# A two-block transformer kernel on one core: gate tiles as split products, their rests on GpSimd, the layer norm one tile sooner

## The chip, the cores and the metric

The kernel runs on one core of one Trainium2 chip. The metric is the device time of one execution in microseconds, as the median of several runs. "Faster" and "slower" are told against the kernel before.

## What is computed

The reference is a float32 network for 256 tokens of width 1024. A first block (a feed-forward part, a mixer with three kinds of attention, a second feed-forward part) is followed by two equal layers. The change touches the mixing stage of these two layers. With `h` the normalised and modulated input of the layer it computes

```python
proj = h @ w_in[l]
u_conv = proj[..., :2 * D_CONV]                      # a: 8 tiles of 128 columns
u_pool = proj[..., 2 * D_CONV:2 * D_CONV + D_POOL]   # p: 4 tiles
gate_a, gate_b = jnp.split(jax.nn.sigmoid(proj[..., 2 * D_CONV + D_POOL:]), N_BRANCHES, axis=-1)  # G: 16 tiles
y_a = conformer_conv_branch(u_conv, conv_w[l], ...)  # a*sigmoid(g), causal depthwise conv of 31 taps, layer norm, silu, matmul
y_b = pool_branch(u_pool, pool_w[l], pool_scale[l])
x = x + g1[:, None, :] * ((gate_a * y_a + gate_b * y_b) @ w_out[l])
```

Behind it stands a mixture of 32 experts, whose weights (192 tiles of 512 KB per layer) are all read from HBM.

## The kernel before, in words

**Weights as a stream.** All weights lie in HBM as tiles of 128 x 1024 float32 (512 KB). `stream()` (line 180) lists them in the order of their use, with a third entry that says whether a tile is split. SyncE loads them in that order (line 753) into a ring of six buffers `raw`; a load of a tile waits until the buffer's last tile has been used: for a split tile until its rest is made (`lo_done`), for a raw one until its product is done (`pe_tile`). Between these loads stand early loads of expert tiles, one beside each of the tiles p and the first gate tiles.

**Split and raw products.** TensorE multiplies rounded numbers (fp32r) in one pass and full float32 in more. A split tile is turned into a high part `whi` (ScalarE's copy, `hi`, line 1651) and a rest `wlo = raw - whi` (VectorE's subtraction, `lo`, line 2105). The activations are split likewise (`hhi`, `hlo`). `product` (line 928) then makes three fp32r products, high x high, high x rest and rest x high, in place of one full product. There are four buffers of each part (`AHEAD = 4`): ScalarE may copy tile n only when the product of tile n - 4 is done, VectorE makes the rest once the copy is there, and TensorE waits for the rest. A raw tile is multiplied as it is: `feature_tile` (line 963) takes `hf` and the loaded tile (line 969) and needs neither ScalarE nor VectorE before the product.

**The mixing stage of a layer.** TensorE goes through 8 tiles a (the first three in step with the activations), 4 tiles p and 16 gate tiles G, each of 8 chunks of 128 x 128 against 256 tokens; a and p are split, G is raw. Then come one split tile `pool`, four split tiles `conv` and eight split tiles `wout`. ScalarE evicts each product (`evac`, line 1662). VectorE in the meantime makes the products a x sigmoid(g) for four groups of channels (line 2658) and the 124 taps of the convolution (`some_taps`, line 2637), one instruction of 256 columns each, with the rests of the tiles a and p between them. After the last tap comes the layer norm: TensorE sums over the channels (line 1452, behind gate tile `LN_MEAN_G`), VectorE subtracts the mean (line 2696), ScalarE squares, TensorE sums again (line 874, behind gate tile `LN_VAR_G`, after a small product for the router, line 1459), a root, VectorE scales (line 2704), ScalarE applies silu and rounds, and VectorE makes the rest (line 2711). Between them VectorE makes the window means of the four pooling groups. While gate tiles 12 to 15 are multiplied, ScalarE and VectorE split the `pool` tile and the first conv tiles. Last, VectorE joins the branches in four steps of two chunks (lines 2718, 2725, 2730, 2733), with one rest of a `wout` tile in each.

**GpSimd** issues five DMAs in the first 421 us and, per layer, waits for a flag of the router and works only if an expert has more tokens than its place holds.

The lines that set the two kinds of products and VectorE's rests inside the taps:

```python
out += [(f"G{l}", m, False) for m in range(16)]     # line 196, in stream()
...
                for m in range(8):
                    lo(NUMBER[START[f"a{l}"] + m] + AHEAD)
                    if m % 2:
                        c = m // 2
                        evacuated(dve, f"a{l}", m)
```

Of the kernel before, what the change touches and what calls it, by code (L numbers as in the profile page):

```python
# [17 lines left out]
F32 = mybir.dt.float32  # L18
# [15 lines left out]
AHEAD = 4  # L34
# [145 lines left out]
def stream():  # L180

    out = [("ffn1", w, True) for w in swiglu_order(FC)]
    out += [("memk", m, True) for m in range(4)] + [("memv", m, True) for m in range(4)]
    out += [("dn", m, True) for m in range(8)] + [("z", m, True) for m in range(4)]
    out += [("dv", m, True) for m in range(4)] + [("kv", m, True) for m in range(4)]
    out += [("v", m, True) for m in range(2)]
    out += [("q", m, True) for m in range(2)] + [("w1", m, False) for m in range(4)] + [("q", m, True) for m in (2, 3)]
    out += [("memq", m, True) for m in range(2)] + [("w1", m, False) for m in range(4, 8)]
    out += [("memq", m, True) for m in (2, 3)]
    out += [("gate", m, True) for m in range(24)]  # L190
    out += [("branch", (m, b), True) for m in range(4) for b in range(3)]
    out += [("wout", m, True) for m in range(DC)]
    out += [("ffn2", w, True) for w in swiglu_order(FC)]
    for l in range(LAYERS):
        out += [(f"a{l}", m, True) for m in range(8)] + [(f"p{l}", m, True) for m in range(4)]
        out += [(f"G{l}", m, False) for m in range(16)]
        out += [(f"pool{l}", 0, True)] + [(f"conv{l}", m, True) for m in range(4)]
        out += [(f"wout{l}", m, True) for m in range(DC)]
        out += [(f"moe{l}", w, False) for w in moe_order()]
    return out  # L200
# [3 lines left out]
SPLITS = [r for r, t in enumerate(STREAM) if t[2]]  # L204
NUMBER = {r: n for n, r in enumerate(SPLITS)}
START = {}
# [157 lines left out]
while len(TAP_ORDER) < 4 * CONV_K:  # L364
    _left = [c for c in range(4) if sum(t[0] == c for t in TAP_ORDER) < CONV_K][:2]
    TAP_ORDER += [(c, sum(t[0] == c for t in TAP_ORDER)) for c in _left]
LN_MEAN_G, LN_VAR_G, SPLIT_G = 10, 11, 16 - AHEAD


NORM_PARTS = [1 if k in (8, 11) else 4 for k in range(8 + 3 * LAYERS)]  # L370
# [142 lines left out]
def program(nc, wstream, ada_d, c_d, consts_d, params_d, x_d, mem_d, rows_d, out_d):  # L513
    with ExitStack() as ctx:
        sems = {}

        def s(name):
            name = SHARED.get(name, (name, 0))[0]
            if name not in sems:
                sems[name] = ctx.enter_context(nc.semaphore(name))  # L520
            return sems[name]

        def after(name, count):

            return SHARED.get(name, (name, 0))[1] + count
# [287 lines left out]
        @block.gpsimd  # L813
        def _(pool):
            pool.wait_ge(s("pe_tile"), 2)
            pool.dma_start(mem_in[:, :], mem_d.rearrange("p c t -> p (c t)")).then_inc(s("mem_loaded"), 16)
            pool.wait_ge(s("pe_tile"), 10)
            pool.dma_start(consts[:, P:], consts_d[:, P:]).then_inc(s("consts_loaded"), 16)
            pool.wait_ge(s("bias_rows"), 1)
            pool.dma_start(rows_d.rearrange("h (j n) c -> (h j) n c", n=HEADS), spread(rt[:, 0:1], (HEADS, BROW), (0, 1))  # L820
                           ).then_inc(s("rows_stored"), 16)
            pool.dma_start(params[:, NFIRST:NPARAM], params_d[:, NFIRST:NPARAM]).then_inc(s("layer_params"), 16)
            pool.wait_ge(s("rows_stored"), 16)

            skew = bass.AP(tensor=rows_d.tensor, offset=P - 1, ap=[[BROW - 1, P], [P * BROW, HEADS], [1, T]])
            pool.wait_ge(s("dn_out"), after("dn_out", 1))
            pool.dma_start(tb[:], skew).then_inc(s("tb_loaded"), 16)

            for l in range(LAYERS):
                pool.wait_ge(s("flag_ready"), after("flag_ready", l + 1))  # L830
                with pool.If(pool.value_load(overflow[0:1, l:l + 1], min_val=0, max_val=1) > 0):
                    pool.wait_ge(s("pe_tile"), START[f"moe{l}"] + 6 * EXPERTS)

                    def unit(u, gu, d, i):
                        if u > 0:
                            pool.wait_ge(s(f"spare_free{l}"), along(u, i, 4))

                        half = slice(512 * (u % 2), 512 * (u % 2) + 512)

                        def tile(r):  # L840
                            at = START[f"moe{l}"] + r
                            src = wstream[at:at + 1, :, half] if i is None else wstream[bass.ds(at + 24 * i, 1), :, half]
                            return src.rearrange("o p c -> (o p) c")
                        for k in range(8):
                            pool.dma_start(gate2[:, 2 * k:2 * k + 2, :].rearrange("p c t -> p (c t)"), tile(gu[k])
                                           ).then_inc(s(f"spare_loaded{l}"), 16)
                        for k in range(4):
                            pool.dma_start(spare_d[:, k % 2, 512 * (k // 2):512 * (k // 2) + 512], tile(d[k])
                                           ).then_inc(s(f"spare_loaded{l}"), 16)
                    spare_units(pool, unit)  # L850
# [797 lines left out]
        def _(act):  # L1648
# [13 lines left out]
            def evac(r, out, bank, func=ACT.Copy):  # L1662
                act.wait_ge(s("pe_tile"), r + 1)
                src = work[bank][:, 0:T]
                if len(out.shape) == 3:
                    src = src.rearrange("p (q f) -> p q f", q=QT)
                assert EVAC[r] == done[0]
                act.activation(out, src, func).then_inc(s("tile_evac"), 1)  # L1668
                done[0] += 1
# [311 lines left out]
            for l in range(LAYERS):  # L1981
# [13 lines left out]
                for m in range(8):  # L1995
# [3 lines left out]
                        act.wait_ge(s("glu_done"), 4 * l + m // 2 - 1)  # L1999
                    evac(r, (pair_a, pair_b)[m % 2][:, (m // 2) % 2, :], m % 4, (ACT.Copy, ACT.Sigmoid)[m % 2])  # L2000
                for m in range(4):
                    evac(START[f"p{l}"] + m, ppad[:, m, 16:16 + T], m % 4)
                for m in range(16):
                    evac(START[f"G{l}"] + m, gate2[:, m, :], m % 4, ACT.Sigmoid)
                    if m == LN_MEAN_G:
                        act.wait_ge(s("ln_centred"), l + 1)
                        act.activation(ln_squares[:, :, :], yconv[:, :, :], ACT.Square).then_inc(s("norm_sq"), 1)
                    elif m == LN_VAR_G:
                        roots(k + 1)
                    if m >= SPLIT_G:  # L2010
                        hi(NUMBER[START[f"pool{l}"]] + m - SPLIT_G)
                    if m == SPLIT_G:
                        act.wait_ge(s("ln_scaled"), l + 1)
                        for c in range(4):
                            a = act.activation(yconv[:, c, :], yconv[:, c, :], ACT.Silu, bias=col(f"ln_b{l}", c),
                                               scale=col(f"ln_g{l}", c))
                        a.then_inc(s("y_silu"), 1)
                        act.wait_ge(s("y_silu"), after("y_silu", l + 1))
                        act.activation(yhi[:, :, :], yconv[:, :, :], ACT.Copy).then_inc(s("y_high"), 1)
# [76 lines left out]
        def _(dve):  # L2096
# [525 lines left out]
            for l in range(LAYERS):  # L2622
# [28 lines left out]
                    tap_at[0] += n  # L2651

                for m in range(8):
                    lo(NUMBER[START[f"a{l}"] + m] + AHEAD)
                    if m % 2:
                        c = m // 2
                        evacuated(dve, f"a{l}", m)
                        dve.tensor_tensor(vpad[:, c, 30:30 + T], pair_a[:, c % 2, :], pair_b[:, c % 2, :], ALU.mult
                                          ).then_inc(s("glu_done"), 1)
                        dve.wait_ge(s("glu_done"), 4 * l + c + 1)  # L2660
                    if m > 0:
                        some_taps(4)
# [41 lines left out]
                dve.tensor_tensor(yconv[:], yconv[:], spread(rstd[:, 0:1], (4, T), (0, 1)), ALU.mult  # L2704
                                  ).then_inc(s("ln_scaled"), 1)
                pooling(3).then_inc(s("pooled"), 1)
                for m in range(SPLIT_G, 16):
                    lo(NUMBER[START[f"pool{l}"]] + m - SPLIT_G)
                    if m == SPLIT_G:
                        dve.wait_ge(s("y_high"), l + 1)  # L2710
                        dve.tensor_tensor(ylo[:], yconv[:], yhi[:].bitcast(F32), ALU.subtract).then_inc(s("y_ready"), 1)
                lo(NUMBER[START[f"pool{l}"]] + AHEAD)

                dve.wait_ge(s("pe_tile"), START[f"pool{l}"] + 1)
                evacuated(dve, f"G{l}", 15)
                for m in range(4):
# [11 lines left out]
                    dve.wait_ge(s("conv_read"), 4 * l + m + 1)  # L2728
                    c = slice(2 * m, 2 * m + 2)
                    dve.tensor_tensor(hf[:, c, :], hf[:, c, :], gate2[:, c, :], ALU.add).then_inc(s("mixed"), 1)  # L2730
                    lo(NUMBER[START[f"conv{l}"] + m] + AHEAD)
                    dve.wait_ge(s("mixed_high"), 4 * l + m + 1)
                    dve.tensor_tensor(hlo[:, c, :], hf[:, c, :], hhi[:, c, :].bitcast(F32), ALU.subtract
# [355 lines left out]
```

## Time and profile before

| | us |
|---|---|
| median of 3 runs | 1586.73 |
| lowest and highest run | 1584.74, 1590.69 |
| profiled execution, its own time | 1583.35 |
| its span | 1581.7 |
| TensorE busy | 1445.7 (91%) |
| VectorE busy | 907.6 (57%) |
| ScalarE busy | 577.4 (37%) |
| GpSimd busy | 3.7 (0%) |

In the profile's rows PE is TensorE, PEld its weight loads, DVE VectorE, ACT ScalarE, POOL GpSimd and SP SyncE. L934 is line 934 of the kernel. Times are us from the span's start unless marked ns. PEclk is the granted TensorE clock as a share of 2.4 GHz. The chain of waits is followed back from the last instruction to what released each; each of its pieces has a start and a length.

### The profile page before, as it was taken

The numbers are of one execution on the slowest core, as the hardware profiler recorded it, in microseconds if no ns is written. First come the engines' busy times: TensorE is split into PE (matmuls) and PEld (weight loads), VectorE is DVE, ScalarE is ACT, GpSimd is POOL, SyncE is SP. The second block draws the span as 40 slices with busy tenths as digits, with TensorE's granted clock in tenths as the row PEclk, the third lists the DMA queues.
The fourth block names the chain that finished last, engine by engine and source line by source line (L and its number), as shares of the span: only waits on it lengthen the run. The fifth ranks groups of instructions, "written<-read, shape, count | busy, mean of one in ns | idle before, by whom it ended". The sixth has DMA issues, their size and how long they took to land.

```text
span 1581.7 us, 26885 instructions
## 1 busy us (share of the span) xinstructions
PE 1445.7 (91%) x10541; PEld 1174.6 (74%) x10553; DVE 907.6 (57%) x1615; ACT 577.4 (37%) x916; POOL 3.7 (0%) x9
## 2 busy tenths in 40 slices
PE   9999999989978899999999999987779999997776
PEld 8999999979877798999999898422217989532222
DVE  6898877684435576888877986210016987410102
ACT  4543346522445554434445153221115143221101
POOL 0000000000000000000000000000000000000000
PEclk9999999999989999999999999999999999899997
DMA  8998854412522344888875558899996749699996
GB/s 303 380 356 310 304 179 147 147 54 107 188 67 95 120 144 163 321 307 299 309 252 192 208 200 346 336 409 409 409 410 258 272 133 378 246 409 409 409 410 252
DMA packets 115803, 420.87 MB, mean 266 GB/s; under 512 B 12944, under 2 KB 13088, under 8 KB 115568
## 3 DMA queue, kind: packets, MB, share of 16 engines
q1 hardware_dynamic: 114624, 414.19, 70.5%
q0 software_dynamic: 1072, 5.20, 0.9%
q8 instruction: 74, 1.21, 0.3%
q14 instruction: 33, 0.27, 0.0%
HBM read 416.71 MB, written 2.62 MB: 265 GB/s over the span
## 4 chain that ended last, share of the span: by engine, by line
PE 68%; DMA 12%; DVE 7%; SPq 5%; ACT 4%; issue 3%; DVEq 0%; ACTq 0%
PE work L934 25%; PE acc L934 12%; PE work L969 7%; SPq L753 5%; PE work L1025 5%; PE work L1570 4%; DMA raw<-wstream_d 3%; DMA over_splits<-wstream_d 3%; DMA hf<-wstream_d 2%; PE work L894 2%; PE work L904 2%; ACT whi L1660 2%; DVE wlo L2110 1%; PE work L1597 1%; DMA over_end<-wstream_d 1%
## 5 line engine op out<-in xcount | busy, mean ns | idle before, releaser
L2110 DVE TENSOR_TENSOR wlo<-raw,whi 128x1024 fp32r<-128x1024 f32 x264 | 321.1, 1223 | 174.6 <-ACT whi L1660 174.1
L1660 ACT ACTIVATE whi<-raw 128x1024 fp32r<-128x1024 f32 x264 | 277.0, 1056 | 278.6 <-PE work L934 190.7
L934 PE MATMUL work<-hhi,whi 128*128 128x256 f32 x1024 | 293.7, 287 | 2.2 <-DVE hlo L2138 1.3
L934 PE MATMUL work<-hlo,whi 128*128 128x256 f32 x1024 | 292.2, 285 | 0.0
L934 PE MATMUL work<-hhi,wlo 128*128 128x256 f32 x1024 | 292.1, 285 | 0.0
L934 PEld LDWEIGHTS work<-hhi,whi 128*128 128x128 f32 x1024 | 198.8, 194 | 4.5 <-DVE wlo L2110 3.0
L934 PEld LDWEIGHTS work<-hlo,whi 128*128 128x128 f32 x1024 | 198.8, 194 | 0.1
L934 PEld LDWEIGHTS work<-hhi,wlo 128*128 128x128 f32 x1024 | 198.6, 194 | 0.0
L2862 DVE TENSOR_TENSOR pair_b<-work,pair_a 128x256 f32<-128x256 f32 x16 | 6.8, 425 | 213.0 <-ACT pair_a L2065 213.0
L2221 DVE SCALAR_TENSOR_TENSOR ada_tiles<-ada_tiles,c_act 128x1024 f32<-128x1024 f32 x96 | 116.3, 1220 | 0.6 <-DMA ada_tiles<-ada_d 0.5
L969 PE MATMUL work<-hf,raw 128*128 128x256 f32 x512 | 111.5, 379 | 0.0
L969 PEld LDWEIGHTS work<-hf,raw 128*128 128x128 f32 x512 | 97.1, 190 | 13.1
L1025 PE MATMUL work<-hhi,whi 128*128 128x256 f32 x288 | 86.7, 301 | 21.0 <-ACT gates L1668 17.8
L934 PE MATMUL acc<-ahi,whi 128*128 128x256 f32 x352 | 99.1, 281 | 2.8 <-DVE alo L2256 2.8
L2646 DVE SCALAR_TENSOR_TENSOR yconv<-vpad,params,yconv 128x256 f32<-128x256 f32 x240 | 99.4, 479 | 1.4
L934 PE MATMUL acc<-alo,whi 128*128 128x256 f32 x352 | 99.6, 283 | 0.0
L934 PE MATMUL acc<-ahi,wlo 128*128 128x256 f32 x352 | 99.4, 282 | 0.0
L1025 PE MATMUL work<-hhi,wlo 128*128 128x256 f32 x288 | 84.6, 294 | 0.0
L1025 PE MATMUL work<-hlo,whi 128*128 128x256 f32 x288 | 84.2, 292 | 0.0
L2048 ACT ACTIVATE xg<-work,mod,gscale 128x256 f32<-128x256 f32 x56 | 29.0, 562 | 140.0 <-PE work L1505 140.0
L1025 PEld LDWEIGHTS work<-hhi,whi 128*128 128x128 f32 x288 | 57.0, 198 | 26.3 <-issue 23.7
L2858 DVE TENSOR_REDUCE rt<-work 32x1 f32<-32x2 f32 x64 | 10.0, 156 | 113.0 <-ACT selectT L2056 111.5
(483 smaller groups left out, 2690.4 us busy)
## 6 DMA issues: line engine op xcount, KB each, us to landing
raw<-wstream_d SPq DMA_DIRECT2D x376, 512.0 KB, 4.8
ada_tiles<-ada_d SPq DMA_DIRECT2D x96, 512.0 KB, 5.2
over_splits<-wstream_d SPq DMA_DIRECT2D x80, 512.0 KB, 15.2
over_select<-wstream_d SPq DMA_DIRECT2D x48, 512.0 KB, 14.8
over_end<-wstream_d SPq DMA_DIRECT2D x24, 512.0 KB, 15.2
spare_d<-wstream_d SPq DMA_DIRECT2D x24, 512.0 KB, 14.7
over_pool<-wstream_d SPq DMA_DIRECT2D x22, 512.0 KB, 15.1
hf<-wstream_d SPq DMA_DIRECT2D x20, 512.0 KB, 15.1
```

What stands on the lines that cost most here:

```text
L753: sp.dma_start(tiles[slot][:], src).then_inc(s(landed(slot)), 16)
L894: mm = pe.matmul(work[bank][:, q:q + 1], hf[:, m, q * P:(q + 1) * P], ones[:, 0:1], start=(m == 0 and q == 0), stop=(m == DC - 1), skip_gr ...
L904: pe.matmul(work[bank][:, :], zero[:, :], spread(zero[:, 0:1], (512,), (0,)), start=True, stop=True)
L934: mm = pe.matmul(out, a, b, start=(start and k == 0), stop=(stop and k == n - 1), skip_group_check=skip)
L969: mm = pe.matmul(work[bank][:, 0:T], h[:, c * P:(c + 1) * P], hf[:, c, :], start=(c == 0), stop=(c == DC - 1))
L1025: mm = pe.matmul(bank[:, 0:T], ((h, h, l)[k % 3])[:, c * P:(c + 1) * P], ((hhi, hlo, hhi)[k % 3])[:, c, :], start=(k == 0), stop=(k == 23))
L1570: mm = pe.matmul(work[0][SLOTS * e:SLOTS * e + SLOTS, :], xg[:, p // 2 % 2, k, a:a + SLOTS], w[:, e % 2 * 512:(e % 2 + 1) * 512], start=(k ...
L1660: act.activation(whi[n % AHEAD][:], tiles[SLOT[SPLITS[n]]][:], ACT.Copy).then_inc(s("hi_done"), 1)
L2048: return act.activation(out, src, ACT.Identity, bias=mod[:, b:b + 1], scale=gscale[:, g:g + 1])
L2110: dve.tensor_tensor(wlo[n % AHEAD][:], tiles[SLOT[SPLITS[n]]][:], whi[n % AHEAD][:].bitcast(F32), ALU.subtract).then_inc(s("lo_done"), 1)
L2221: dve.scalar_tensor_tensor(ada_tiles[:, k, :], ada_tiles[:, k, :], 1.0, c_act[:], ALU.mult, ALU.mult, accum_out=out).then_inc(s("ada_done" ...
L2646: ins = dve.scalar_tensor_tensor(yconv[:, c, :], vpad[:, c, i:i + T], w, yconv[:, c, :], ALU.mult, ALU.add)
```

## The change

The gate tiles of both layers become split tiles. So each needs a copy on ScalarE (`hi` before its eviction, as for the tiles p now too) and a rest. The rests of the tiles from a4 to conv3 (29 per layer: 4 a, 4 p, 16 G, pool, 4 conv) are made by GpSimd in a loop `rests`; VectorE's calls for 13 tiles go. VectorE still makes the rests of a0 to a3 and of the `wout` tiles; before the first of these it waits until GpSimd has ended its last. The mean of the layer norm is summed behind gate tile 9 in place of 10, the variance behind 10 in place of 11.

```diff
--- before.py
+++ after.py
@@ -193,7 +193,7 @@
     out += [("ffn2", w, True) for w in swiglu_order(FC)]
     for l in range(LAYERS):
         out += [(f"a{l}", m, True) for m in range(8)] + [(f"p{l}", m, True) for m in range(4)]
-        out += [(f"G{l}", m, False) for m in range(16)]
+        out += [(f"G{l}", m, True) for m in range(16)]
         out += [(f"pool{l}", 0, True)] + [(f"conv{l}", m, True) for m in range(4)]
         out += [(f"wout{l}", m, True) for m in range(DC)]
         out += [(f"moe{l}", w, False) for w in moe_order()]
@@ -364,7 +364,7 @@
 while len(TAP_ORDER) < 4 * CONV_K:
     _left = [c for c in range(4) if sum(t[0] == c for t in TAP_ORDER) < CONV_K][:2]
     TAP_ORDER += [(c, sum(t[0] == c for t in TAP_ORDER)) for c in _left]
-LN_MEAN_G, LN_VAR_G, SPLIT_G = 10, 11, 16 - AHEAD
+LN_MEAN_G, LN_VAR_G, SPLIT_G = 9, 10, 16 - AHEAD
 
 
 NORM_PARTS = [1 if k in (8, 11) else 4 for k in range(8 + 3 * LAYERS)]
@@ -826,7 +826,16 @@
             pool.wait_ge(s("dn_out"), after("dn_out", 1))
             pool.dma_start(tb[:], skew).then_inc(s("tb_loaded"), 16)
 
+            def rests(first, end):
+
+                pool.wait_ge(s("lo_done"), first)
+                for n in range(first, end):
+                    pool.wait_ge(s("hi_done"), n + 1)
+                    pool.tensor_tensor(wlo[n % AHEAD][:], tiles[SLOT[SPLITS[n]]][:], whi[n % AHEAD][:].bitcast(F32),
+                                       ALU.subtract).then_inc(s("lo_done"), 1)
+
             for l in range(LAYERS):
+                rests(NUMBER[START[f"a{l}"]] + AHEAD, NUMBER[START[f"wout{l}"]])
                 pool.wait_ge(s("flag_ready"), after("flag_ready", l + 1))
                 with pool.If(pool.value_load(overflow[0:1, l:l + 1], min_val=0, max_val=1) > 0):
                     pool.wait_ge(s("pe_tile"), START[f"moe{l}"] + 6 * EXPERTS)
@@ -1999,16 +2008,16 @@
                         act.wait_ge(s("glu_done"), 4 * l + m // 2 - 1)
                     evac(r, (pair_a, pair_b)[m % 2][:, (m // 2) % 2, :], m % 4, (ACT.Copy, ACT.Sigmoid)[m % 2])
                 for m in range(4):
+                    hi(NUMBER[START[f"p{l}"] + m] + AHEAD)
                     evac(START[f"p{l}"] + m, ppad[:, m, 16:16 + T], m % 4)
                 for m in range(16):
+                    hi(NUMBER[START[f"G{l}"] + m] + AHEAD)
                     evac(START[f"G{l}"] + m, gate2[:, m, :], m % 4, ACT.Sigmoid)
                     if m == LN_MEAN_G:
                         act.wait_ge(s("ln_centred"), l + 1)
                         act.activation(ln_squares[:, :, :], yconv[:, :, :], ACT.Square).then_inc(s("norm_sq"), 1)
                     elif m == LN_VAR_G:
                         roots(k + 1)
-                    if m >= SPLIT_G:
-                        hi(NUMBER[START[f"pool{l}"]] + m - SPLIT_G)
                     if m == SPLIT_G:
                         act.wait_ge(s("ln_scaled"), l + 1)
                         for c in range(4):
@@ -2651,7 +2660,6 @@
                     tap_at[0] += n
 
                 for m in range(8):
-                    lo(NUMBER[START[f"a{l}"] + m] + AHEAD)
                     if m % 2:
                         c = m // 2
                         evacuated(dve, f"a{l}", m)
@@ -2704,12 +2712,8 @@
                 dve.tensor_tensor(yconv[:], yconv[:], spread(rstd[:, 0:1], (4, T), (0, 1)), ALU.mult
                                   ).then_inc(s("ln_scaled"), 1)
                 pooling(3).then_inc(s("pooled"), 1)
-                for m in range(SPLIT_G, 16):
-                    lo(NUMBER[START[f"pool{l}"]] + m - SPLIT_G)
-                    if m == SPLIT_G:
-                        dve.wait_ge(s("y_high"), l + 1)
-                        dve.tensor_tensor(ylo[:], yconv[:], yhi[:].bitcast(F32), ALU.subtract).then_inc(s("y_ready"), 1)
-                lo(NUMBER[START[f"pool{l}"]] + AHEAD)
+                dve.wait_ge(s("y_high"), l + 1)
+                dve.tensor_tensor(ylo[:], yconv[:], yhi[:].bitcast(F32), ALU.subtract).then_inc(s("y_ready"), 1)
 
                 dve.wait_ge(s("pe_tile"), START[f"pool{l}"] + 1)
                 evacuated(dve, f"G{l}", 15)
@@ -2728,6 +2732,8 @@
                     dve.wait_ge(s("conv_read"), 4 * l + m + 1)
                     c = slice(2 * m, 2 * m + 2)
                     dve.tensor_tensor(hf[:, c, :], hf[:, c, :], gate2[:, c, :], ALU.add).then_inc(s("mixed"), 1)
+                    if m == 0:
+                        dve.wait_ge(s("lo_done"), NUMBER[START[f"wout{l}"]])
                     lo(NUMBER[START[f"conv{l}"] + m] + AHEAD)
                     dve.wait_ge(s("mixed_high"), 4 * l + m + 1)
                     dve.tensor_tensor(hlo[:, c, :], hf[:, c, :], hhi[:, c, :].bitcast(F32), ALU.subtract
```

## Rows read from the trace of the kernel before

**Rows 1.** The page: span, then busy time, share and instructions of the engines

```profile
span 1581.7 us, 26885 instructions
...
PE 1445.7 (91%) x10541; PEld 1174.6 (74%) x10553; DVE 907.6 (57%) x1615; ACT 577.4 (37%) x916; POOL 3.7 (0%) x9
```

**Rows 2.** The chain of waits in both layers' mixing stages: start, us, what

```profile
840.30 34.55 PE work L934 x288
874.86 37.99 PE work L969 x176
912.85 1.73 PE work L1452 x8
914.57 3.45 PE work L969 x16
918.02 1.71 PE work L1459 x16
...
921.54 13.81 PE work L969 x64
935.35 2.83 PE acc L934 x24
938.18 11.31 PE work L934 x96
...
1243.13 37.99 PE work L969 x176
```

**Rows 3.** Windows: length, busy time of the engines, clock, DMA share, GB/s

```profile
874.86:912.85 37.99, 37.99 (x177) 33.44 (x177) 37.48 (x94) 4.23 (x11) 0.00 (x0) 1.00 0.52 184
...
975.10:1000.00 24.90, 22.26 (x162) 15.49 (x166) 15.26 (x65) 8.39 (x16) 0.00 (x0) 0.93 0.60 227
1000.00:1198.40 198.40, 159.38 (x988) 55.56 (x982) 22.30 (x59) 35.47 (x69) 0.00 (x0) 0.95 1.03 408
```

**Rows 4.** VectorE's timeline in the first layer: start, length, what [idle before, releaser]

```profile
852.33 0.43 DVE L2658 TENSOR_TENSOR vpad<-pair_a,pair_b 128x256 f32<-128x256 f32 x1 [0.47 <-ACT pair_b L1668]
...
871.09 12.49 DVE L2646 SCALAR_TENSOR_TENSOR yconv<-vpad,params,yconv 128x256 f32<-128x256 f32 x31
...
890.21 21.66 DVE L2646 SCALAR_TENSOR_TENSOR yconv<-vpad,params,yconv 128x256 f32<-128x256 f32 x52
912.02 0.53 DVE L2668 TENSOR_TENSOR vpad<-params,gscale 128x144 f32<-128x144 f32 x2 [0.15 <-DVE yconv L2646]
...
930.87 1.23 DVE L2711 TENSOR_TENSOR yp<-yconv,yp 128x1024 fp32r<-128x1024 f32 x1 [0.38 <-ACT yp L2019]
```

**Rows 5.** ScalarE's timeline in the first layer

```profile
848.31 1.06 ACT L1660 ACTIVATE whi<-raw 128x1024 fp32r<-128x1024 f32 x1 [3.60 <-PE work L934]
...
864.40 0.36 ACT L1668 ACTIVATE pair_b<-work 128x256 f32<-128x256 f32 x1
...
878.35 0.38 ACT L1668 ACTIVATE gate<-work 128x256 f32<-128x256 f32 x1 [3.07 <-PE work L969]
```

**Rows 6.** Instruction groups of VectorE from 852.3 to 912: busy us, mean ns

```profile
L2646 DVE SCALAR_TENSOR_TENSOR yconv<-vpad,params,yconv 128x256 f32<-128x256 f32 x120 | 49.7, 478 | 0.7
L2110 DVE TENSOR_TENSOR wlo<-raw,whi 128x1024 fp32r<-128x1024 f32 x6 | 7.3, 1220 | 0.0
```

**Rows 7.** GpSimd's instruction groups over the span, the longest and a constant

```profile
L827 POOL DMA_DIRECT2D tb<-bias_rows_d x1 | 0.9, 909 | 334.3 <-DVEq L2516 334.3
...
L3081 POOL MEMSET const-float32-1.0<- 128x1 f32 x1 | 0.1, 98 | 0.0
```

**Rows 8.** VectorE's reciprocal of the layer norm, in its timeline

```profile
922.80 1.75 DVE L2123 RECIPROCAL rstd<-std 128x256 f32<-128x256 f32 x1 [0.48 <-ACT std L1693]
```

**Rows 9.** VectorE's timeline in the first step of the joining

```profile
940.51 0.87 DVE L2718 SCALAR_TENSOR_TENSOR hf<-acc,params,gate 128x256 f32<-128x256 f32 x2
...
944.07 0.69 DVE L2733 TENSOR_TENSOR hlo<-hf,hhi 128x512 fp32r<-128x512 f32 x1
```

**Rows 10.** Windows of a gap in the expert stage and of the routing

```profile
1039.00:1040.00 1.00, 0.00 (x0) 0.00 (x0) 0.00 (x0) 0.00 (x0) 0.00 (x0) 1.00 1.02 406
...
988.00:990.00 2.00, 2.00 (x11) 2.00 (x11) 1.69 (x10) 1.13 (x2) 0.00 (x0) 0.50 0.01 4
```

## The prediction

> **What bounds the kernel now.** I read four views of the layer that begins near 840 us; the second layer repeats them 368.3 us later with the same lengths, as its first gate part shows beside layer one's [rows 2]. First the page: TensorE is busy for 91% of the span [rows 1]. Then the chain of waits [rows 2]: from 840.30 to 949.49 us every piece is TensorE's own work and no other engine stands in it. The reader is to see two tile prices there. Twelve split tiles (a, p) take 34.55 us, 2.879 us each; eleven raw gate tiles take 37.99 us, 3.454 us each. Third the windows [rows 3]: during the gate tiles the clock is 1.00 and DMA half idle (0.52), and behind the mixing stage the expert loads run at 408 GB/s and bound the next 198 us, but only after a stretch at 0.60, where they wait for buffers and not for bandwidth. Fourth VectorE's timeline [rows 4]: its last tap ends at 911.87, just before TensorE asks for it at 912.85. So both engines are close to the path, and the change shortens both.
>
> **Part 1, gate tiles split.** Each of 16 gate tiles goes from 3.454 to 2.879 us: 16 x 0.575 = 9.2 us less on TensorE per layer. The two price tags are of the same engine at the same clock, so this term is firm. ScalarE gets 16 more copies of 1.06 us [rows 5]; it sits idle 3.07 us before each gate eviction [rows 5] and they fit there (2.88 - 0.38 leaves 2.5). A load of a weight tile into a buffer that held a gate tile now waits for that tile's rest and no longer for its product, so no tile comes later; SyncE's queue gets no new instruction.
>
> **Part 2, rests on GpSimd.** VectorE loses 13 of its 1.22 us rests per layer, of which six lie inside the tap stretch, 7.3 us [rows 6]. How long GpSimd takes for one 128x1024 subtraction T no row shows: in this trace GpSimd only issues a few DMAs and sets constants [rows 7]. Bounds: the same instruction on VectorE, 1.22 us [rows 6], and the dearest element in the trace, the reciprocal's 1.75 us for 256 elements, 7.0 us for 1024 [rows 8]. I take 2.4 us, twice the row with the same operation and shape, as the nearer end; what matters is only on which side of three limits it falls. (a) The rest of a4: ScalarE's copy runs 848.31 to 849.37 [rows 5], the product needs it when a3 ends, 874.86 - 8 x 2.879 = 851.83, so 2.46 us are free: cost 0, at T = 2.88 about 0.4. (b) Steady state: T must stay under 2.88 us, or GpSimd sets the pace. (c) The new wait of VectorE at the first mixed pair: ScalarE copies the last conv tile after the pool product, GpSimd ends some 3.5 us behind that product (4.6 if it is one rest behind), while VectorE gets to its wait 4.4 us behind it (conv0's 2.83, then 0.9 and 0.7). Cost 0 to 0.2 us, and queued behind it are only VectorE's first rest for the out projection and its second half, which TensorE needs 11.3 us after the pool product [rows 2]. The first pair takes from 940.51 to 944.76 today [rows 9]; the slack stays.
> The Trainium skill ("GPSIMD Engine Reference", section "3.1 Elementwise — side-by-side cycle accounting") measures such an operation at 1.96 times VectorE's time for twice this length. By that ratio an estimate from our 1.22 us row is 2.4 us, and the sum stays as it is; no run here shows it yet.
>
> **Part 3, VectorE's taps and the earlier layer norm.** The last product of the a stage that the taps need is evicted at 864.40 + 0.36 = 864.76 [rows 5]. Before it VectorE has from 852.33 only 24 taps and three gate products (24 x 0.41 + 3 x 0.45 = 11.2 us), so it stands ready at 863.5; today the rests keep it busy until 871.09 [rows 4]. The 100 taps behind it take 911.87 - 871.09 = 40.8 us [rows 4]. So the taps end at 864.8 + 0.45 + 40.8 = 906.0, 5.9 us sooner. TensorE finishes gate tile 9, where the mean now stands, at 874.86 + 10 x 2.88 = 903.7. It waits 2.4 us, with nothing else in its queue to do: +2.4 us. From the mean on the length is unchanged: today 22.50 us to the last gate tile (mean 1.73, one tile 3.45, router row and squares 3.52, four tiles 13.81) [rows 2]; after it 1.73 + 2.88 + 3.52 + 5 x 2.88 = 22.5. VectorE's chain from the last tap to the split layer norm output takes 932.1 - 911.9 = 20.2 us [rows 4], so it ends near 926, and TensorE asks at 931.4. Not on the path.
>
> **Sum.** Per layer -9.2 + 2.4 = -6.8 us; the expert stage starts so much sooner, and as its loads wait for buffers that TensorE frees, it shifts whole. Two layers: -13.6 us. The profiled execution took 1583.35 us, which gives 1569.8; it lies 3.4 us under the median of the runs, so I forecast a median of 1573. Own range of this case: 1565 (hardly any wait before the mean, 4.8 us better) to 1579 (0.4 us at a4, and the wait costing clock). On the clock: a gap of 1.2 us leaves it at 1.00, but in the routing stretch with its thin products it falls to the 1.2 GHz level [rows 10]; a few us at that level after the 2.4 us wait would cost 1 to 3 us per layer.
>
> **Rival 1, slower: the two engines can't both read.** Place: the 100 taps, each with two inputs from SBUF, while GpSimd reads two others. If a rest holds VectorE for h us, 21 rests (a5 to gate 13) come before the mean is free; 1.3 us of that falls into VectorE's idle time at 863.5. Taps end at 906.0 + 21h - 1.3. The gain of 9.2 is used up when they end at 912.85, at h = 0.39 us. With h = 1.22 they end at 930.3, TensorE waits 26.6 us, +17.4 per layer: 1583.35 + 34.9 + 3.4 = 1621.6. For it: VectorE's rate on two inputs, 0.41 us for 256 columns, is one column a cycle with little to spare, and its path has no slack left (2.4 us negative). Against it: no row of this trace shows two engines slowing each other, ScalarE and VectorE run side by side all along.
> The Trainium skill ("SBUF — State Buffer", "Summary: rules for kernel authors") speaks against this change: a VectorE instruction with two SBUF inputs and a GpSimd one that reads SBUF exclude each other, the later one waiting for the whole of the earlier. With the ratio above h would be 2.4 us and the estimate 1671; the trace has no GpSimd arithmetic to agree or not. I give this rival 0.27, and a weak form with h of 0.2 to 0.5 another 0.05, which ends within 0.5%.
>
> **Rival 2: GpSimd sets the pace.** For T above 2.88 us, 29 rests cost 29 x (T - 2.88) per layer, in place of the 2.4 us wait: break-even at T = 3.20. T between 3.06 and 3.33 gives within 8 us of no change; T = 3.45 gives +7.3 per layer, 1601. For it: the range of T reaches to 7.0. Against: only the reciprocal is so slow. Chance 0.18, 0.10 of it without a measurable difference and 0.08 slower.
>
> **Rival 3: the gain is swallowed.** If the expert stage is paced by bandwidth from further back (the loads of the mixing stage included), 6.8 us sooner on TensorE only lengthen its waits there, and the time stays at 1587. Against it the 0.60 stretch before the saturated one [rows 3]. Chance 0.05.
>
> **How the numbers follow.** What a measurement can tell here is about 0.5%, 7.9 us. The forecast with its variants has 0.45, all faster by more than that. Within 0.5%: 0.05 + 0.10 + 0.05 = 0.20. Slower: 0.27 + 0.08 = 0.35. The likeliest single case gives the number, 1573. The range goes from 1563, a bit under the own range, to 1650, which holds rival 1 up to h of about 1.9 and rival 2 up to T of 4.3; it leaves out the dearer third of rival 1 and the far end of rival 2.
>
> **What would show it.** Raw products are gone from line 969; the gate tiles take 2.88 us each in the chain. GpSimd has 58 subtractions. Right: VectorE's taps stay at 0.41 us apart and end 5.9 us sooner, and TensorE has one wait of 2 to 3 us per layer before the mean, on VectorE. Rival 1: taps in the same 480 ns shape take far longer in mean or with gaps, the last ending after 912, and a long TensorE wait in front of the mean. Rival 2: gaps between all tiles from a4 on, ended by GpSimd, with starts more than 2.88 us apart. Rival 3: the gate stretch shorter as said, and DMA waits in the expert stage longer by as much. Any of these would make the forecast wrong, as would an expert stage that doesn't shift whole.

## The result and the profile after

| | before | after |
|---|---|---|
| median, us | 1587.36 | 1670.67 |
| lowest and highest, us | 1584.74, 1590.69 | 1666.98, 1671.49 |
| span of the profiled execution | 1581.7 | 1669.8 |
| TensorE busy | 1445.7 | 1446.2 |
| VectorE busy | 907.6 | 980.0 |

The change makes the kernel slower: ratio 1.0524, interval 1.0507 to 1.0542, five runs of each. The forecast of 1573 with its range up to 1650 was wrong, in sign too. Rival 1 gave 1622 if a rest takes h = 1.22 us from VectorE, and 1671 with h = 2.4.

The page of after, its engines [rows 1] and the slices of the clock (tenths of 2.4 GHz):

```profile
span 1669.8 us, 27499 instructions
...
PE 1446.2 (87%) x10797; PEld 1180.3 (71%) x10809; DVE 980.0 (59%) x1589; ACT 606.4 (36%) x948; POOL 148.8 (9%) x67
...
PEclk8999999899989999999999599999979859999996
```

VectorE lost 26 rests of 1.22 us and yet is busy 72 us longer. TensorE has the same busy time in a longer span, so it waits somewhere. The waits of TensorE by line (us in total, times, longest) say where:

```profile
PE work L1461 <- DVEq L2673: 88.5, 2, 44.3
```

That is the mean of the layer norm, waiting for the taps, 44.2 us per layer. The instruction groups of after say what the taps suffer:

```profile
L2655 DVE SCALAR_TENSOR_TENSOR yconv<-vpad,params,yconv 128x256 f32<-128x256 f32 x240 | 170.6, 775 | 1.4
L834 POOL TENSOR_TENSOR wlo<-raw,whi 128x1024 fp32r<-128x1024 f32 x58 | 145.0, 2531 | 838.3 <-ACT whi L1669 837.8
L2666 DVE TENSOR_TENSOR vpad<-pair_a,pair_b 128x256 f32<-128x256 f32 x8 | 15.6, 1956 | 13.0 <-ACT pair_b L1677 13.0
```

The taps, 478 ns in [rows 6], have a mean of 775 ns. But a mean hides the pattern; the two timelines of the first layer show it. GpSimd's (start, length, what):

```profile
854.77 17.38 POOL L834 TENSOR_TENSOR wlo<-raw,whi 128x1024 fp32r<-128x1024 f32 x7 [435.00 <-ACT whi L1669]
875.77 38.04 POOL L834 TENSOR_TENSOR wlo<-raw,whi 128x1024 fp32r<-128x1024 f32 x15 [3.62 <-ACT whi L1669]
```

and VectorE's, against [rows 4]:

```profile
857.63 2.19 DVE L2666 TENSOR_TENSOR vpad<-pair_a,pair_b 128x256 f32<-128x256 f32 x1 [6.61 <-ACT pair_b L1677]
859.86 2.39 DVE L2651 TENSOR_SCALAR yconv<-vpad,params 128x256 f32<-128x256 f32 x1
...
888.74 20.36 DVE L2655 SCALAR_TENSOR_TENSOR yconv<-vpad,params,yconv 128x256 f32<-128x256 f32 x8
...
932.71 21.67 DVE L2655 SCALAR_TENSOR_TENSOR yconv<-vpad,params,yconv 128x256 f32<-128x256 f32 x52
```

Read these three steps together. While GpSimd has no pause (875.77 to 913.81, 38.04 / 15 = 2.54 us a rest), eight taps take 20.36 us, 2.54 us each: **one tap per rest**. When GpSimd is idle, 52 taps take 21.67 us, 0.417 each, as before. A rest thus takes 2.54 - 0.417 = 2.12 us from VectorE. The Trainium skill ("SBUF — State Buffer", section "Who interferes with whom") says that the two engines share one pair of ports, as an exclusive lock held for a whole instruction; these timelines agree, with 2.54 us for 256 columns that need 0.42.

The chain of after, from the first tiles of the layer to the out projection, answers to [rows 2]:

```profile
845.54 8.65 PE work L943 x72
...
954.49 3.64 PE work L1461 x8
958.12 2.88 PE work L943 x24
...
962.47 1.97 PE work L1468 x16
964.45 3.22 PE work L883 x8
967.67 14.63 PE work L943 x120
982.29 2.83 PE acc L943 x24
985.12 11.31 PE work L943 x96
```

**Where the time went.** The layer begins at 845.54 in place of 840.30, 5.2 us of the profiled execution that lie ahead of the first instruction that the change touches. (In the traces here this start lies between 840.3 and 846.8; one trace per kernel doesn't tell whether that belongs to the kernel or to the execution.) With that taken off, the mean begins 954.49 - 912.85 - 5.24 = 36.4 us later than before, and from the mean to the end of gate tile 15 it takes 982.29 - 954.49 = 27.8 us in place of 22.5. Both together are 41.7 us per layer; 2 x 41.7 + 5.2 = 88.6, against 88.1 us by which the spans differ. The medians differ by 83.3 us, which is 2 x 41.7 nearly to the tenth. The pieces from conv0 to the out projection have the lengths of before.

The 5.3 us behind the mean are a second cost of the wait. The windows of after (length, busy PE, PEld, DVE, ACT, POOL, clock, DMA share, GB/s):

```profile
920.00:940.00 20.00, 0.00 (x0) 0.00 (x0) 19.93 (x52) 0.00 (x0) 0.00 (x0) 0.50 0.00 0
...
954.00:958.00 4.00, 3.51 (x9) 2.86 (x10) 2.87 (x9) 0.00 (x0) 0.00 (x0) 0.52 0.00 0
958.00:961.00 3.00, 3.00 (x25) 2.79 (x23) 2.62 (x6) 1.06 (x1) 0.00 (x0) 1.00 0.04 8
```

TensorE stands still, the granted clock falls to its 1.2 GHz level, and the mean runs at that level: 3.64 us in place of 1.73.

### The profile page after: what moved, and what is told of

Same layout as the page of the kernel before. It is cut to its first block, busy times and chain, and to the rows that moved or that the text cites. A ratio compares the mean times of both kernels' runs of the same rounds, so it can differ in the third digit from the quotient of the medians.

```text
span 1669.8 us, 27499 instructions
## 1 busy us (share of the span) xinstructions
PE 1446.2 (87%) x10797; PEld 1180.3 (71%) x10809; DVE 980.0 (59%) x1589; ACT 606.4 (36%) x948; POOL 148.8 (9%) x67
## 4 chain that ended last, share of the span: by engine, by line
PE 57%; DVE 16%; DMA 11%; SPq 7%; ACT 5%; issue 4%; DVEq 0%; ACTq 0%
PE work L943 24%; PE acc L943 11%; DVE yconv L2655 10%; SPq L753 7%; PE work L1034 5%; DMA hf<-wstream_d 3%; PE work L1579 3%; DMA raw<-wstream_d 2%; DMA ln_squares<-wstream_d 2%; ACT whi L1669 2%; PE work L903 2%; PE work L913 1%; PE work L1606 1%; DMA c_act<-wstream_d 1%; DMA over_vpad<-wstream_d 1%
## 5 line engine op out<-in xcount | busy, mean ns | idle before, releaser
L1669 ACT ACTIVATE whi<-raw 128x1024 fp32r<-128x1024 f32 x296 | 310.9, 1057 | 315.2 <-PE work L943 228.8
L2119 DVE TENSOR_TENSOR wlo<-raw,whi 128x1024 fp32r<-128x1024 f32 x238 | 289.2, 1223 | 163.0 <-ACT whi L1669 162.4
L943 PE MATMUL work<-hhi,whi 128*128 128x256 f32 x1280 | 368.7, 288 | 2.9 <-POOL wlo L834 0.9
L943 PE MATMUL work<-hlo,whi 128*128 128x256 f32 x1280 | 364.8, 285 | 0.0
L943 PE MATMUL work<-hhi,wlo 128*128 128x256 f32 x1280 | 364.4, 285 | 0.0
L943 PEld LDWEIGHTS work<-hhi,whi 128*128 128x128 f32 x1280 | 248.7, 194 | 6.6 <-DVE wlo L2119 2.5
L943 PEld LDWEIGHTS work<-hlo,whi 128*128 128x128 f32 x1280 | 248.6, 194 | 0.5
L943 PEld LDWEIGHTS work<-hhi,wlo 128*128 128x128 f32 x1280 | 248.3, 194 | 0.0
L834 POOL TENSOR_TENSOR wlo<-raw,whi 128x1024 fp32r<-128x1024 f32 x58 | 145.0, 2531 | 838.3 <-ACT whi L1669 837.8
L2655 DVE SCALAR_TENSOR_TENSOR yconv<-vpad,params,yconv 128x256 f32<-128x256 f32 x240 | 170.6, 775 | 1.4
L1034 PE MATMUL work<-hhi,whi 128*128 128x256 f32 x288 | 88.1, 306 | 21.0 <-ACT gates L1677 17.8
L1034 PE MATMUL work<-hhi,wlo 128*128 128x256 f32 x288 | 85.8, 298 | 0.0
L1034 PE MATMUL work<-hlo,whi 128*128 128x256 f32 x288 | 85.7, 298 | 0.0
L1034 PEld LDWEIGHTS work<-hhi,whi 128*128 128x128 f32 x288 | 58.2, 202 | 26.1 <-issue 24.0
```

The costliest lines, as they stand in the source:

```text
L834: pool.tensor_tensor(wlo[n % AHEAD][:], tiles[SLOT[SPLITS[n]]][:], whi[n % AHEAD][:].bitcast(F32), ALU.subtract).then_inc(s("lo_done"), 1)
L943: mm = pe.matmul(out, a, b, start=(start and k == 0), stop=(stop and k == n - 1), skip_group_check=skip)
L1034: mm = pe.matmul(bank[:, 0:T], ((h, h, l)[k % 3])[:, c * P:(c + 1) * P], ((hhi, hlo, hhi)[k % 3])[:, c, :], start=(k == 0), stop=(k == 23))
L1669: act.activation(whi[n % AHEAD][:], tiles[SLOT[SPLITS[n]]][:], ACT.Copy).then_inc(s("hi_done"), 1)
L2119: dve.tensor_tensor(wlo[n % AHEAD][:], tiles[SLOT[SPLITS[n]]][:], whi[n % AHEAD][:].bitcast(F32), ALU.subtract).then_inc(s("lo_done"), 1)
L2655: ins = dve.scalar_tensor_tensor(yconv[:, c, :], vpad[:, c, i:i + T], w, yconv[:, c, :], ALU.mult, ALU.add)
```

## The experiments

Experiments 5 and 7 start from the kernel before, the others from the kernel after. Ratios are to the kernel before, timed on the same chip.

**1. Gate tiles raw again, the other rests on GpSimd.** The mean stands behind tile 10 again, and GpSimd makes the 13 rests of a layer that VectorE made before.

```diff
-        out += [(f"G{l}", m, True) for m in range(16)]
+        out += [(f"G{l}", m, False) for m in range(16)]
...
-LN_MEAN_G, LN_VAR_G, SPLIT_G = 9, 10, 16 - AHEAD
+LN_MEAN_G, LN_VAR_G, SPLIT_G = 10, 11, 16 - AHEAD
...
-                    hi(NUMBER[START[f"G{l}"] + m] + AHEAD)
```

> The changed kernel with the gate tiles raw again and the mean behind tile 10: GpSimd makes 13 rests per layer, 8 of them (a4 to p3) while the taps run. Theory L (a GpSimd subtraction and a VectorE instruction with SBUF inputs exclude each other, one VectorE instruction passing per rest): the after trace has the taps end 43.2 us later than my 906.0 for 21 rests, 2.06 us each; 8 rests give 906.0 + 8 x 2.1 - 1.3 = 921.5, so TensorE waits some 8.7 us before the mean and the time is about 1587 + 17 = 1604. Theory G (the gate tiles' splitting is what costs: ScalarE's copies, the clock or the order of waits): then this kernel is at 1587, and its taps stay 480 ns.

1611.21 us, 1.0138 (1.0114 to 1.0163). The groups:

```profile
L2655 DVE SCALAR_TENSOR_TENSOR yconv<-vpad,params,yconv 128x256 f32<-128x256 f32 x240 | 119.6, 565 | 1.4
...
L834 POOL TENSOR_TENSOR wlo<-raw,whi 128x1024 fp32r<-128x1024 f32 x26 | 63.7, 2481 | 856.8 <-ACT whi L1669 856.8
```

Slower with not one gate tile split: eight rests of a layer stand beside the taps, and TensorE waits 5.2 us before each mean. So the use of GpSimd alone costs, and with 8 of its instructions beside the taps in place of 22 it costs less. The wait had been expected at 8.7 us and the time near 1604. Behind the wait the mean takes 3.78 us in place of 1.73 and the tile 4.52 in place of 3.45. Wait and both make 8.3 us per layer; the time rose by 22 us in all, so some 5 us are not explained.

**2. GpSimd only writes.** It writes zeros in place of the rests; the low part of 29 weight tiles per layer is left out of the computation.

```diff
-                    pool.tensor_tensor(wlo[n % AHEAD][:], tiles[SLOT[SPLITS[n]]][:], whi[n % AHEAD][:].bitcast(F32),
-                                       ALU.subtract).then_inc(s("lo_done"), 1)
+                    pool.memset(wlo[n % AHEAD][:].bitcast(F32), 0.0).then_inc(s("lo_done"), 1)
```

> The changed kernel in which GpSimd fills the rest tiles with zeros in place of the subtraction (the 58 rests are left out of the result), so that it writes the same 128x1024 but reads nothing. Theory L in the form of a shared input path: taps back at 480 ns, TensorE's wait before the mean near 2.4 us, time 1573. Theory L with any GpSimd work holding VectorE: each fill of about 1 us holds a tap by its length, taps' mean above 550 ns and the time above 1600. Theory G: near 1670, as nothing in the waits changes.

1578.81 us, 0.9945 (0.9924 to 0.9967), 92 us below after. Its groups, then its waits of TensorE:

```profile
L2654 DVE SCALAR_TENSOR_TENSOR yconv<-vpad,params,yconv 128x256 f32<-128x256 f32 x240 | 99.1, 479 | 1.4
...
L834 POOL MEMSET wlo<- 128x1024 f32 x58 | 55.4, 954 | 832.5 <-ACT whi L1668 832.5
```

```profile
PE work L1460 <- DVEq L2672: 5.0, 2, 2.5
...
PE work L1467 <- ACT gate L1676: 3.0, 2, 1.5
```

An engine that reads nothing beside the taps leaves them at 479 ns. This is nearly the forecast's case, with the collision gone (GpSimd is also quicker than forecast, 0.95 us in place of 2.4), and it lets the rest of the sum be read: TensorE waits 2.5 us before the mean, where the forecast had 2.4. But the gain is not 13.6 us, it is 8.7 (0.0055 x 1586, with the interval 5.2 to 12.1); why is seen in its chain:

```profile
914.69 0.92 ACT ln_squares L2017
915.65 1.05 ACT whi L1668
916.71 0.28 ACT gate L1676
917.03 1.98 PE work L1467 x16
919.00 2.94 PE work L882 x8
921.94 14.89 PE work L942 x120
```

The router's product waits 1.5 us for the eviction of gate tile 10. That eviction stands in ScalarE's queue behind the squares, and now also behind the new copy of a tile, 1.05 us, that a raw tile did not need. Then the variance takes 2.94 us in place of 1.81, in a window with the clock at 0.59 (919 to 922). From the mean, at 910.7, to the end of the gates at 936.83 it takes 26.1 us, not 22.5: 3.6 per layer that the forecast did not have. With them its sum would give 13.6 - 2 x 3.6 = 6.4 us, inside the interval.

**3. Shorter instructions on GpSimd.** The same rests in four parts of 256 columns.

```diff
+                    for j in range(4):
+                        a = slice(j * T, (j + 1) * T)
+                        ins = pool.tensor_tensor(wlo[n % AHEAD][:, a], tiles[SLOT[SPLITS[n]]][:, a],
+                                                 whi[n % AHEAD][:, a].bitcast(F32), ALU.subtract)
+                    ins.then_inc(s("lo_done"), 1)
```

> The changed kernel with each GpSimd rest made in four instructions of 256 columns. Theory L, exclusion for the length of one instruction: no tap longer than about 1.2 us (a quarter of 2.5 plus its own 0.48) where now they reach 2.6, four taps pass per rest; GpSimd's turns take 4 x (0.65 + 0.41) = 4.2 us per tile, over TensorE's 2.88, so TensorE has gaps before tiles from a5 on; the sum of both engines' work until the mean is the same, so time within 1650 to 1690. Rival (the two engines share bandwidth and both slow down evenly): taps keep their long shape of around 2 us.

1664.76 us, 1.0481 (1.0453 to 1.0509). Its group on GpSimd and its waits of TensorE:

```profile
L836 POOL TENSOR_TENSOR wlo<-raw,whi 128x256 fp32r<-128x256 f32 x232 | 194.0, 874 | 777.8 <-ACT whi L1672 777.8
```

```profile
PE work L1464 <- DVEq L2676: 58.7, 2, 29.4
...
PE work L946 <- POOL wlo L836: 12.7, 34, 0.6
```

And its taps in VectorE's timeline, beside the eight of after:

```profile
873.97 7.00 DVE L2658 SCALAR_TENSOR_TENSOR yconv<-vpad,params,yconv 128x256 f32<-128x256 f32 x8
```

A tap now takes 7.00 / 8 = 0.875 us, as long as one GpSimd instruction of 0.874. So the hold lasts one GpSimd instruction, whatever its length, and one VectorE instruction passes between two of them. Four holds of 0.875 - 0.417 = 0.46 us take 1.8 us per rest from VectorE in place of 2.12, so the total hardly falls. The wait before the mean shrinks to 29.4 us mostly because TensorE comes to it later: four parts together take GpSimd 4 x 0.87 = 3.5 us, longer than the 2.88 us of a product, so GpSimd now sets the pace of the gate tiles: rival 2's mechanism, made by the experiment.

**4. The running sum of the taps in PSUM.** A tap then has one input in SBUF and one in PSUM, and all the rests stay on GpSimd. The last tap of a channel group writes SBUF.

```diff
-                            ins = dve.scalar_tensor_tensor(yconv[:, c, :], vpad[:, c, i:i + T], w, yconv[:, c, :],
+                            ins = dve.scalar_tensor_tensor(yconv[:, c, :] if i == CONV_K - 1 else acc_c[:, c, :],
+                                                           vpad[:, c, i:i + T], w, acc_c[:, c, :],
```

> The changed kernel with the taps' running sum in PSUM (the part of acc that is free then), only the last tap of each group writing to SBUF: each tap has one SBUF input in place of two, GpSimd's subtractions stay. Theory L with the second SBUF input as what collides: taps of about 480 ns, only the four gate products (two SBUF inputs) are held for up to 2.5 us each; TensorE's wait before the mean 2 to 10 us; time 1573 to 1588. If any SBUF read of VectorE collides, the time stays near 1670. Theory G: 1670 too.

1594.36 us, 1.0039 (1.0018 to 1.0060), 76 us below after. Its group of taps, and its timeline of VectorE:

```profile
L2655 DVE SCALAR_TENSOR_TENSOR acc<-vpad,params,acc 128x256 f32<-128x256 f32 x232 | 95.7, 484 | 1.3
```

```profile
858.87 2.19 DVE L2667 TENSOR_TENSOR vpad<-pair_a,pair_b 128x256 f32<-128x256 f32 x1 [6.58 <-ACT pair_b L1677]
861.10 0.55 DVE L2651 TENSOR_SCALAR acc<-vpad,params 128x256 f32<-128x256 f32 x1
...
869.22 1.68 DVE L2667 TENSOR_TENSOR vpad<-pair_a,pair_b 128x256 f32<-128x256 f32 x1
870.93 3.23 DVE L2655 SCALAR_TENSOR_TENSOR acc<-vpad,params,acc 128x256 f32<-128x256 f32 x8
...
886.81 0.48 DVE L2655 SCALAR_TENSOR_TENSOR yconv<-vpad,params,acc 128x256 f32<-128x256 f32 x1
```

GpSimd still takes 2464 ns for each of its 58 rests, and the taps run through it at 484 ns. What has two inputs in SBUF, the product a x sigmoid(g), is held as before, up to 2.19 us in place of 0.43 [rows 4]; TensorE waits 6.1 us per layer, and the time is above the 1573 to 1588 that were expected. The last row tells input from output: the last tap of a group reads its sum from PSUM and writes SBUF, a rest of GpSimd runs from 885.87 to 888.27, and the tap still takes 0.48 us. So what holds a tap is its second input in SBUF, not its output there.

**5. The control: the same edit of the taps in the kernel before.**

> Control for e4: the kernel before (raw gates, all rests on VectorE, nothing on GpSimd) with the taps' running sum in PSUM. If the PSUM form costs or gains nothing by itself (taps of 484 ns in e4 against 480), the time is 1587 within 0.5%; if it is what brought e4 back by 76 us, this kernel would be far faster than 1587.

1585.56 us, 0.9987 (0.9969 to 1.0006), taps 484 ns. The form in PSUM is neutral without GpSimd; all that it gains in experiment 4 is the collision.

**6. The layer norm where it was.** After, with the mean behind tile 10 and the variance behind 11 (one line, as in experiment 1).

> The changed kernel with part 3 undone: mean behind gate tile 10, variance behind 11. Theory L: the mean still waits for the last tap; TensorE does one more tile (2.9 us) before the wait, but GpSimd one more rest (2.1 us held) too, so the gain per layer is below 1 us: 1666 to 1672. If the earlier mean were a cost of its own of several us, the time would fall by over 5 us.

1668.26 us, 1.0506 (1.0474 to 1.0538), against 1.0524 (1.0507 to 1.0542) of after; TensorE waits 43.6 us before the mean. The earlier mean has no measurable part in the loss.

**7. The gates split, no GpSimd.** VectorE makes all the rests, 16 more than before, four taps between two of them. The mean stands behind tile 13, and ScalarE's silu behind tile 15, so that TensorE has other work meanwhile.

```diff
+                for j in range(16):
+                    lo(NUMBER[START[f"G{l}"]] + j)
+                    some_taps(4)
```

> Part 1 alone: gate tiles split, all rests on VectorE (16 more per layer, each followed by four taps), GpSimd unused, the mean behind tile 13, where VectorE can be ready. Theory L says VectorE's time is what pays in either case, 1.13 us per rest of its own against 2.1 us held by GpSimd: taps end near 852.3 + 53 + 24 x 1.13 = 932 in place of 954 (after), and the chain of the layer norm, 20 us, then sets the start of conv near 952 in place of 938: +14 per layer, time 1610 to 1622, slower than before but about 50 us faster than the changed kernel. If the splitting as such cost what the change lost, this would be near 1670.

1625.61 us, 1.0228 (1.0200 to 1.0257), a little above the span that was expected and 45 us below after. Its chain, inside the gates:

```profile
907.02 1.13 DVE wlo L2110
908.15 1.59 DVE yconv L2646 x4
...
934.40 3.78 PE work L1452 x8
```

A rest on VectorE costs VectorE 1.13 us; a rest on GpSimd costs VectorE 2.12. Handing the work over takes nearly twice as much from the engine that it was to relieve.

**8. GpSimd with one input.** It copies the raw tile in place of subtracting; the result is no rest, so the values of the layers are others, the router's too.

```diff
+                    pool.tensor_copy(wlo[n % AHEAD][:], tiles[SLOT[SPLITS[n]]][:]).then_inc(s("lo_done"), 1)
```

> The changed kernel in which GpSimd copies the raw tile into the rest tile in place of the subtraction (the rests are left out of the result): one input is read, 128x1024, and as much written. The hold per rest should be the copy's own length: if the copy takes 1.0 to 1.3 us, taps meet it with up to 1.5 us, 21 x (1.1 - 0.4) = 15 to 20 us later taps in place of 43, time 1600 to 1620. If reading one tensor does not hold VectorE, the taps stay at 480 ns and the time is that of e2, 1579.

2918.22 us, 1.8404. Its groups on GpSimd show why this time says nothing on the question:

```profile
L853 POOL DMA_DIRECT2D gate<-wstream_d x256 | 137.1, 538 | 1293.6 <-PE acc L1648 874.4 <-PE work L1605 256.4 <-issue 154.4
...
L834 POOL CAST wlo<-raw 128x1024 fp32r<-128x1024 f32 x58 | 65.4, 1128 | 634.8 <-ACT whi L1668 634.6
```

The DMAs of line 853 belong to the path for an expert with too many tokens; in after GpSimd has its 58 rests and nine other instructions, and none of these. Only the mixing stage can be read, in VectorE's groups and in the chain:

```profile
L2654 DVE SCALAR_TENSOR_TENSOR yconv<-vpad,params,yconv 128x256 f32<-128x256 f32 x240 | 129.5, 602 | 1.4
```

```profile
858.09 1.32 DVE yconv L2654
...
859.44 1.19 DVE yconv L2654
...
860.66 0.49 DVE yconv L2654
```

A copy of 1.13 us holds a tap too, up to 1.32 us: one read by GpSimd is enough. The hold is shorter because the instruction is. And since this copy and the zeros of experiment 2 (1.13 and 0.95 us) are of nearly one length and write the same tile, it is GpSimd's read that makes the difference, not its length or its write.

**9 and 10. What is left of the idea.** Taps in PSUM, GpSimd's rests only up to gate tile 15, VectorE makes those of pool and conv as before. The mean stands behind tile 10 in the first, behind 11 in the second.

```diff
-                rests(NUMBER[START[f"a{l}"]] + AHEAD, NUMBER[START[f"wout{l}"]])
+                rests(NUMBER[START[f"a{l}"]] + AHEAD, NUMBER[START[f"pool{l}"]])
```

> e4 (split gates, taps in PSUM, GpSimd) with two edits: the mean behind tile 10, and GpSimd's rests end with gate tile 15 (24 per layer), VectorE again makes those of pool and conv as before the change, so that GpSimd is quiet while VectorE runs the window means and the joining. Theory L: the taps end where they do in e4 (9.8 us behind my 900-line: 6.1 us of wait becomes 3.2), no held instruction in the window means but those beside the rests of tiles 14 and 15, no wait of VectorE in the joining: 5 to 8 us per layer better than e4, 1594 - 10..16 = 1578 to 1584, just under the kernel before. If it stays at 1590 or above, the layer norm's chain of VectorE and ScalarE is the bound and not GpSimd's holds.

> e7 with the mean behind gate tile 11 and the variance behind 12. TensorE's wait before the mean falls to about 0.3 us, which saves its clock, but the chain from the last tap to the layer norm's output (20 us and more) then ends after TensorE has done the pool product, so up to 4 us per layer are lost there: within 4 us of e7, either side.

Behind 10: 1583.41 us, 0.9969 (0.9954 to 0.9983), a little faster than before and the lowest median here of the kernels that compute the whole reference. It is not clear of experiment 5, the kernel before with its taps in PSUM (1585.56, on the same chip; the runs of the two overlap). So a gain from split gates and GpSimd as such is not shown. Behind 11: 1590.36, 1.0020 (0.9995 to 1.0044), no difference from before, and 7 us above the first where at most 4 had been expected. The chain of the first:

```profile
914.42 2.45 PE work L1461 x8
916.88 3.96 PE work L943 x24
...
924.35 11.72 PE work L943 x96
```

Its gates are split and cheap, yet the wait before the mean is 3.2 us, and the mean and the tile behind it run partly at the lower clock, 2.45 and 3.96 us in place of 1.73 and 2.88. So 1.8 of the 9.2 us per layer go there, on top of the wait. With the mean one tile later TensorE waits 0.4 us for the taps, but the chain then runs through VectorE's layer norm, and in it through a window mean that is held beside the last rest of GpSimd, for 2.32 us in place of 0.29:

```profile
913.73 2.32 DVE L2696 TENSOR_SCALAR rt<-pair_a 128x256 f32<-128x256 f32 x1
```

From the first tile of the layer to conv0 it takes 94.7 us with the mean behind 11, 91.5 with the mean behind 10, and 95.1 in the kernel before: the gain is returned.

## Why the prediction was wrong

- **The step that failed is in Part 2:** GpSimd's rests were costed at nothing for VectorE, so that Part 3 could end the taps at 906.0. They ended at 954.4, and TensorE waited 44.2 us in place of 2.4. Nothing in the trace of before could show it, as the text said; the step should have carried h as an unknown cost of its own, bounded from nothing to the whole of T. Instead the two halves of that range were split into forecast and rival, and the rival that named place, price and rule got 0.27 against 0.45. The argument used against it, that VectorE and ScalarE run side by side, is about another pair of engines and says nothing of this one.
- **Rival 1** came true in kind. Its formula with h = 2.12 and the profiled execution's 5.2 us gives 906.0 + 44.5 - 1.3 + 5.2 = 954.4, the end that was measured. Its 1671 fits so well partly by chance: h was 2.12 and not 2.4 (one tap passes per rest), 12 us less over two layers, and the 5.3 us per layer behind the mean, which it had not, brought 11 back.
- **Part 1** held: 2.88 us per gate tile. It missed one spot, where the new copy delays an eviction that TensorE waits for (1.5 us, experiment 2).
- **T** was taken as 2.4 us; GpSimd takes 2.40 beside taps that don't collide (experiment 9, from 880.76 on) and 2.54 beside those that do. So (b) held and rival 2 fell. The ratio of the Trainium skill ("GPSIMD Engine Reference", section "3.1 Elementwise — side-by-side cycle accounting"), 1.96, agrees with this trace: 2.40 against 1.22 us. No wait of VectorE at the first mixed pair showed up as a cost, so (c) held; but the pair is ready 3.8 us before TensorE needs it and no longer 4.7, so the slack did not quite stay.
- **Part 3:** the 2.4 us wait was right once the collision was gone (2.5, experiment 2). The stretch behind the mean was mis-sized: 26.1 us, not 22.5. The clock after a short wait had been given 1 to 3 us per layer in words, but was left out of the sum.
- **Rival 3** fell: the expert stage shifted nearly whole. From conv0 to the next layer's first tile it takes 275.6 us in after and 273.4 in experiment 2, whose mixing stage is 3.0 us shorter than before, in place of 273.2. In experiments 1, 4 and 10 it takes 277.5 to 277.8; why is not shown.
- **The lower end of the own range**, 1565, is 4.8 us below the profiled execution's 1569.8 and not below the median's 1573; on that footing it is 1568. The 1563 of the stated range leans on it; the outcome lies at the other end.
- Even without the collision the gain would have been 8.7 us, 0.5%, not 13.6: just what a measurement here can tell.

Left open: a version that also keeps the four products a x sigmoid(g) from reading two SBUF inputs was not tried; by experiment 4 they are held for some 4 x 1.2 us per layer.

## What to carry to other kernels

Before work goes to an idle engine, ask what each instruction of the busy one reads at the same time: here a GpSimd instruction that reads SBUF and a VectorE one with two SBUF inputs exclude each other, so the price to VectorE is GpSimd's duration less one short instruction (2.12 us), more than doing the work itself (1.13). If the work must go there, move one input of the VectorE instructions to PSUM first, or give GpSimd only writes. And when a rule names such a collision and the trace has nothing on it, put its cost into the sum.

## What the runs showed of the hardware that was not expected

- **Strict alternation.** Between two queued GpSimd instructions exactly one VectorE instruction passes, for parts of 1024 and of 256 columns alike. GpSimd hardly suffers: 2.54 us in place of 2.40. The window means of pooling, of two SBUF inputs too, were held the same way in after (2.52 and 2.53 us at 972.49 and 975.04).
- **A one-input instruction can be held too.** The first tap, a multiply and add of one SBUF input by per-partition values, took 2.39 us with its output in SBUF (after) and 0.55 with it in PSUM (experiment 4), as without GpSimd (0.54, experiment 5). Where GpSimd is idle the same instruction takes 0.41 us with its output in SBUF.
- **A wait costs once more in clock.** Waits before the mean of 3.2, 5.2, 15.0 and 44.2 us (experiments 9, 1, 7 and after) were followed by a mean of 2.45, 3.78, 3.78 and 3.64 us in place of 1.73. So the wait of 5.2 us took as much from the mean as the one of 44.2, about 2 us.
